# Weight tiles split earlier, a modulation ring kept through two stages, tables loaded in the opening, and the MLP's gate on VectorE, in a two-layer transformer kernel

## The reference, cut to what matters

```python
mx = jnp.split(cond_x @ ada_w[i] + ada_b[i], 6, axis=-1)
hx = modulate(rms_norm(x, g[0]), mx[0], mx[1])
...
x = x + mx[2] * rms_norm(ox, g[1])
x = x + mx[5] * rms_norm(sq_relu_mlp(modulate(rms_norm(x, g[2]), mx[3], mx[4]),
                                     ff_w1[i], ff_w2[i]), g[3])
```

## Time and profile before

| | us |
|---|---|
| three runs | 3427.12, 3431.72, 3430.05 |
| median | 3430.05 |
| the profiled execution | 3428.0 |
| its span, first to last instruction | 3426.2 |
| its mean granted clock | 0.982 |

### The profile page before, as it was taken

The page is one execution under the profiler, slowest core; times in us unless marked ns, Lnnn a source line. Parts: engine busy times, 40 slices in busy tenths (PEclk is TensorE's granted clock), DMA queues, the critical chain, the costliest instruction groups (busy, mean ns, idle before and its releaser), DMA issues. The chain is left out here.

```text
span 3426.2 us, 39368 instructions
## 1 busy us (share of the span) xinstructions
PE 3290.3 (96%) x15248; PEld 2428.1 (71%) x15248; DVE 1898.6 (55%) x2428; ACT 1285.7 (38%) x2110; POOL 695.5 (20%) x383
## 2 busy tenths in 40 slices
PE   6999999999999999999999999888999999999998
PEld 3664445555888888888999878653457788888886
DVE  3335444433756765664685534577685654445444
ACT  4333444445543323332454222552113533333232
POOL 0001777665431001300220100110012410002001
PEclk8999999999999999999999999999999999999999
DMA  5626333322454454543465311102413432333333
GB/s 221 238 100 236 65 61 78 85 54 73 152 169 131 140 171 137 172 148 94 155 194 160 119 44 39 45 38 106 183 31 117 135 129 93 98 94 125 117 96 105
DMA packets 146651, 406.64 MB, mean 119 GB/s; under 512 B 25498, under 2 KB 39610, under 8 KB 143649
## 3 DMA queue, kind: packets, MB, share of 16 engines
q1 hardware_dynamic: 146464, 404.11, 36.9%
HBM read 345.05 MB, written 58.92 MB: 118 GB/s over the span
## 5 line engine op out<-in xcount | busy, mean ns | idle before, releaser
L1734 PE MATMUL psum<-hid_high,w_high_and_low 128*128 128x512 f32 (+1 forms) x1536 | 416.6, 356 | 7.0 <-DVE hid_low L1983 4.9
L1717 PE MATMUL psum<-h_high,w_high_and_low 128*128 128x512 f32 (+1 forms) x1536 | 415.8, 356 | 0.0
L2005 POOL TENSOR_TENSOR squares_then_rstd_of_out<-squares_then_rstd_of_out,square_out 128x512 f32<-128x512 f32 (+1 forms) x69 | 105.4, 1528 | 1275.8 <-ACT square_out L1804 1275.8
L1789 ACT ACTIVATE w_high_and_low<-w_raw 128x1024 fp32r<-128x1024 f32 x226 | 238.7, 1056 | 326.5 <-PE psum L1734 228.1
L1887 DVE TENSOR_TENSOR w_high_and_low<-w_raw,w_high_and_low 128x1024 fp32r<-128x1024 f32 x226 | 283.3, 1254 | 83.2 <-ACT w_high_and_low L1789 82.4
L1415 POOL TENSOR_TENSOR probs_added<-probs_added,probs_turned 128x1024 f32<-128x1024 f32 x128 | 308.2, 2408 | 67.2 <-ACT probs_turned L1340 54.6
L1734 PEld LDWEIGHTS psum<-hid_high,w_high_and_low 128*128 128x128 f32 x1536 | 274.3, 190 | 50.3 <-DVE hid_low L1983 4.5
L1382 DVE TENSOR_REDUCE row_max<-psum 128x1 f32<-128x1280 f32 x120 | 179.0, 1492 | 229.1 <-PE psum L1278 137.2
L1717 PEld LDWEIGHTS psum<-h_high,w_high_and_low 128*128 128x128 f32 x1536 | 272.8, 189 | 43.8 <-issue 3.7
L1980 DVE TENSOR_TENSOR hid_high<-hid_relu_and_square 128x512 fp32r<-128x512 f32 (+1 forms) x160 | 113.8, 711 | 318.2 <-ACT hid_relu_and_square L1874 317.8
L1734 PE MATMUL psum<-hid_low,w_high_and_low 128*128 128x512 f32 (+1 forms) x768 | 272.3, 355 | 0.0
(11 more groups left out here) (490 smaller groups left out, 6704.8 us busy)
## 6 DMA issues: line engine op xcount, KB each, us to landing
w_raw<-in_ff_w_dram SPq DMA_DIRECT2D x320, 512.0 KB, 3.6
ada_ring<-in_ada_w_dram SPq DMA_DIRECT2D x12, 2048.0 KB, 15.2
ada_rows_in<-in_ada_w_dram SPq DMA_DIRECT2D x96, 256.0 KB, 3.6
w_raw<-in_w_out_dram SPq DMA_DIRECT2D x38, 512.0 KB, 3.6
scratch_spectra<-spectrum_out SPq DMA_DIRECT2D x32, 256.0 KB, 2.0
filter_ring<-scratch_spectra SPq DMA_DIRECT2D x16, 512.0 KB, 4.0
stream_in<-scratch_x SPq DMA_DIRECT2D x27, 256.0 KB, 4.1
w_raw<-in_w_hy_dram SPq DMA_DIRECT2D x12, 512.0 KB, 3.8
```

The lines of the kernel that those rows point to most:

```text
L1717: mm = pe.matmul(bank[:, 0:n], x[i % SLOTS][:, k, :], y[:, k, a:a + n], start=(k == 0 and m == 0), stop=(k == KT - 1 and m == 2))
L1734: mm = pe.matmul(bank[:, 0:n], x[i % SLOTS][:, 2 * k + half, :], y[:, k, 0:n], start=(k == 0 and m == 0), stop=(k == HT - 1 and m == 2))
L1789: act.activation(w_hi[i % SLOTS], raw[i % 2], ACT.Copy).then_inc(w_rounded, 1)
L2005: pool.tensor_tensor(acc_out[:, q % 2, 0:n], acc_out[:, q % 2, 0:n], sq_out[:, v % 2, 0:n], ALU.add).then_inc(added_out, 1)
```

## The change

Four edits. The first weight tiles are loaded ahead of the second chunk of x, rounded by ScalarE ahead of that chunk's squares, and split by VectorE inside the scaling of the chunks. One `Modulation` with one ring serves both stages: SyncE issues its loads of pieces 4 to 6 of the list in the opening, and the projection multiplies the first of them in step 0. `by_head`, `swap` and `cos_a` are loaded in the opening; `sin_a` remains in the projection, with a semaphore of its own. Pieces 10 and 11, the MLP's gate, leave the ring and become a first batch of `ModulationRows` in layer 0's MLP, whose gating waits for it.

```diff
-ADA_LATER = [(0, piece) for piece in range(4, ADA_PIECES)]
-ADA_IN_MLP = [(1, (2, 3), BOTH), (1, (0, 1), BOTH)] + [(1, (4, 5, 6, 7), LATENT), (1, (8, 9, 10, 11), LATENT)]
+ADA_LATER = [(0, piece) for piece in range(4, 10)]
+ADA_IN_MLP = [(0, (10, 11), BOTH), (1, (2, 3), BOTH), (1, (0, 1), BOTH)] + [(1, (4, 5, 6, 7), LATENT), (1, (8, 9, 10, 11), LATENT)]
...
                 ada.load(sp, 1)
+                for t in range(2):
+                    sp.dma_start(g.first_raw[:, t], d["w_qk"][t]).then_inc(w_first, 16)
                 load_x(1)
                 ada.load(sp, 2)
-                for t in range(2):
-                    sp.dma_start(g.first_raw[:, t], d["w_qk"][t]).then_inc(w_first, 16)
                 ada.load(sp, 3)
                 load_x(2)
+                for dst, src in ((g.by_head, "by_head"), (g.swap, "swap_a"), (g.cos_a, "cos_a")):
+                    sp.dma_start(dst[:], d[src]).then_inc(g.tabs_in, 16)
+                for i in range(NEEDED, NEEDED + ada.SLOTS):
+                    ada.load(sp, i)
...
                 scale(0, BACK)
-                scale(1, range(KT))
-                ada.bias(dve, 2)
-                split_off(0, FRONT)
-                split_off(1, FRONT)
                 for t in range(2):
                     dve.wait_ge(w_rounded, t + 1)
                     dve.tensor_tensor(g.first_low[:, t], g.first_raw[:, t], g.first_high[:, t], ALU.subtract).then_inc(w_split, 1)
+                scale(1, FRONT)
+                ada.bias(dve, 2)
+                scale(1, BACK)
+                split_off(0, FRONT)
+                split_off(1, FRONT)
                 ada.bias(dve, 3)
...
-                ada.load_selector(sp)
-                for dst, src in ((by_head, "by_head"), (swap, "swap_a"), (cos, "cos_a"), (sin, "sin_a")):
-                    sp.dma_start(dst[:], d[src]).then_inc(tabs_in, 16)
+                sp.dma_start(sin[:], d["sin_a"]).then_inc(sine_in, 16)
                 ring.load(sp, 2, qk_piece(2))
-                for i in range(ada.SLOTS):
-                    ada.load(sp, i)
                 for u, (t, a, n) in enumerate(units):
-                    if u + 1 >= ADA_FROM:
-                        ada.load(sp, u + 1 - ADA_FROM + ada.SLOTS)
+                    ada.load(sp, ADA_DONE + ada.SLOTS + u)
...
-                    ada.turn(pe, step - ADA_FROM - 1)
-                    if step >= ADA_FROM:
-                        ada.multiply(pe, step - ADA_FROM)
+                    if step:
+                        ada.turn(pe, ADA_DONE + step - 1)
+                    ada.multiply(pe, ADA_DONE + step)
...
-                dve.wait_ge(tabs_in, 64)
+                dve.wait_ge(tabs_in, 48)
+                dve.wait_ge(sine_in, 16)
...
                     if k == 0:
                         dve.wait_ge(rstd_out, q + 1)
+                        if ADA and q == C:
+                            dve.wait_ge(ada.folded, ada.folds_by(of_gate[-1]))
```

More of the change, by code:

```diff
@@ L152, in copy @@
             act.wait_ge(self.turned, i - len(self.banks) + 1)
-        act.activation(self.rows[:, i % len(self.banks), :], self.bank(i), ACT.Copy).then_inc(self.copied, 1)
+        act.activation(self.rows[:, i % 2, :], self.bank(i), ACT.Copy).then_inc(self.copied, 1)
     def turn(self, pe, i):
@@ L161, in turn @@
         for m in range(BANK // P):
-            mm = pe.matmul(self.bank(i)[:, 2 * m:2 * m + 2], self.rows[:, i % len(self.banks), m * P:(m + 1) * P], self.sel[:], start=True, stop=True)
+            mm = pe.matmul(self.bank(i)[:, 2 * m:2 * m + 2], self.rows[:, i % 2, m * P:(m + 1) * P], self.sel[:], start=True, stop=True)
         mm.then_inc(self.turned, 1)
@@ L596, in _ @@
                 for step in range(U + 3):
-                    ada.copy(act, step - ADA_FROM - 1)
+                    if step:
+                        ada.copy(act, ADA_DONE + step - 1)
                     if step < U and step % C == 1:
@@ L1535, in out_and_mlp @@
                 loads_at.setdefault(0 if done is None else min(i for i in rows_at if rows_at[i][-1] >= done) + 1, []).append(m)
[L1536 removed]
+            of_norm = [b for b, (of_layer, of_pieces, streams) in enumerate(ADA) if of_layer > layer and of_pieces[0] < 4]
+            of_gate = [b for b, (of_layer, of_pieces, streams) in enumerate(ADA) if of_layer == layer]
             bank_of = lambda i: g.ps[:, unit_of[i, "ada"] % BANKS, :]
@@ L3222, in build_program @@
         g.first_high, g.first_low = (tile_r(nc, g.first_ring, f"w_{x}", [P, 2, KT, P]) for x in ("high", "low"))
+        g.ada_memory = ExitStack()
+        g.by_head, g.swap = tile(nc, g.ada_memory, "ones_by_head", [P, P]), tile(nc, g.ada_memory, "swap_halves", [P, P])
+        g.cos_a, g.tabs_in = tile(nc, g.ada_memory, "cos_a", [P, TOK]), nc.alloc_semaphore("tables_in")
+        ada_sems = [nc.alloc_semaphore(n) for n in "ada_in0 ada_in1 ada_in2 sel_in made copied turned biased folded".split()]
+        g.ada = Modulation(nc, g, d, g.ada_memory, ada_sems, ADA_FIRST + ADA_LATER, (6, 7))
         opening(nc, g, d)
```

37 lines of the change are left out of this document (18 added, 19 removed).

## The result

The changed kernel takes 3435.85 us (median of 20 runs, 3432.20 to 3439.64) where the kernel before takes 3429.89 us (median of 20). The ratio is 1.0016, with a 95% interval of 1.0010 to 1.0022: slower by 6 us, small but clear of 1, inside the 0.2% that I had called no change, and inside the forecast's range. It is just outside the 4 us around 3431.5 us that I gave a chance of 0.55. The terms behind it were of both signs and most of them nearly as large as forecast. The profiled execution took 3434.41 us, its span 3432.6. One execution of a later kernel (e11) took 8391.69 us and is left out of every comparison.

What follows compares the result with a forecast made beforehand. TensorE, busy 96% of the span, was taken to bound the kernel. Terms of -1.8, +2.7, -14.45, +5.6, +10.05, +2.5, +2.0 and -5.1 summed to +1.5 us, 3431.5 us; eight-in-ten range 3423.5 to 3438.5.

Steps and rivals of the forecast that it cites:

- the 4 us around 3431.5 us: Whole kernel: the forecast time as summed, to be met within 4 us, chance 0.55.
- The bound: Whole kernel: TensorE is busy 96% of the span, so edits count only through its work or few waits.
- The opening (-1.8): Start of kernel: weights loaded and rounded earlier let PE's first product start at 48.6 us, 1.8 us sooner.
- T3 (+2.7): Projection's first product: modulation work fills the gap ahead of it without shortening it; the low clock costs 2.7 us.
- B + 14.1: Projection's first product placed 14.1 us behind the stage's start, against 14.0 before, without the clock's price.
- The ring after T3 and the two waits (-14.45 + 18.15): Projection after its first product: fewer multiplies and turns save 14.45 us; two late ring loads and low clock cost 18.15.
- The low clock: Projection's late ring loads: half-speed work costs 2.2 us within the second wait and 2.5 us behind it.
- the landing: Projection's ring loads: each lands 7.4 us after issue, with bounds of 5.0 and 15.2 us.
- The MLP (+2.0): Layer 0's MLP: VectorE's gate work hides in its waits; PE's extra sum and turn cost 2.0 us.
- The bank (-5.1): Start of project_mamba: a shifted PSUM bank removes the first product's wait and keeps the clock high, saving 5.1 us.
- The rival in which the wait stays: Start of project_mamba: VectorE's clearing or the second weight tile holds PE anyway; +5.1 us, 3436.6 us, chance 0.08.
- The sum: Whole kernel: all terms together give +1.5 us, 3431.5 us on the median, no change that shows.

Runs made afterwards that it cites:

- e11: The changed kernel with the ring's last two pieces multiplied in steps 6 and 8 instead of 4 and 5, SyncE's order untouched: 3413.48 us, ratio 0.9957.
- e10: e5 plus three unread TensorE products in the opening's gap, where PE waits for the later chunk's squares: 3407.53 us, ratio 0.9940.
- e5: e1 with the projection's head sum made ahead of the ring's turn and multiply in each step: 3411.68 us, ratio 0.9946.
- e7: The changed kernel with the ring's next load issued ahead of its unit's two stores, still behind the wait for the low part: 3436.46 us, ratio 1.0021.
- e2: The kernel before with only the third dt sum's PSUM bank changed, to bank 1: 3424.10 us, ratio 0.9984.
- e4: The kernel before with only the MLP's gate (last two pieces) moved from the ring to VectorE in layer 0's MLP: 3421.43 us, ratio 0.9974.
- e9: e4 with VectorE's additions for the gate cut to 64 of 512 columns, leaving out part of the computation: 3418.93 us, ratio 0.9973.
- e1: The changed kernel with the ring loads of the 9th and 10th piece issued ahead of the first store: 3417.45 us, ratio 0.9961.
- e3: The kernel before with by_head, swap and cos_a loaded in the opening, sin_a alone in the projection, ring of squares 4 deep: 3425.39 us, ratio 0.9985.

## Why the prediction was right or wrong

**The bound** was right: each edit counted where it moved PE's waits or its clock, and VectorE's and ScalarE's added work showed only through them.

**The opening (-1.8) was wrong; it measured -0.1.** The step that failed was "the squares, PE's sums and the root all come 2.5 us later". The sums came 2.5 us later and lasted 2.6 us longer, because the clock fell in the idle stretch that the later chunk made for PE. I had priced the clock at the first product and not here. e10 is the test: with that stretch filled the sum takes 7.03 us and the barrier comes 1.9 us sooner than in e5. Against the kernel before, e10's first product is 1.1 us sooner (49.32) and its barrier 1.4 (72.34), most of the forecast's 1.8. In e7, whose opening is that of the changed kernel, the clock stood until 29.4 and the sum took 8.62 us; the first product came at 49.96 and, with the clock up sooner behind it (0.67 in 52 to 54 us, 0.50 before), the barrier at 72.31. So a part of the term is there in some executions. The Trainium skill, TensorE: Matmul & The Clock Gate, Part 1, says that the point of change varies between runs; these traces agree (28.0 and 29.4 us under the same instructions).

One reading at the head of the prediction is wrong as well: `sin_a` is not PE's only long wait in the first 300 us. PE waits 11.0 us ahead of its first sum of squares, and 5.4 at the turn of the earlier trace rows. No edit touches the first of them.

**T3 (+2.7) was right in mechanism**: +3.3, the gap filled and not shortened, and the low clock in it (2.69 and 3.54 us for multiplies of 1.92). My order of events had it at B + 14.1 without the clock's price; e5 shows what held it there, the head sum behind two multiplies. The size is good to a microsecond or so only: in the profiled executions T3 lay 12.3 to 14.0 us behind the barrier where `sin_a` was waited for (before, e2, e4, e9), and 17.3 to 18.8 in the kernels with the ring kept in the changed kernel's order.

**The ring after T3 and the two waits (-14.45 + 18.15) were right in mechanism.** Forecast +3.7 from T3 to the stage's end, measured +3.1. e1 parts the two: without the late loads that stretch takes 96.03 us, 15.7 less than before, and the late loads add 18.8. That 18.8 is so near to 18.15 is partly luck, by two errors that offset each other. The idle time itself was forecast as 5.6 and 7.85 us (10.05 less the 2.2 of the clock), 13.45 together, and measured 6.63 and 9.38, 16.0 together. The low clock was put at 2.2 + 2.5 = 4.7 us, and 2.8 are left for it.

The mis-sized part of the waits is the landing. The first load was issued 13.2 us behind T3, as forecast; only its 7.4 us were too short. I had read them from the DMA engines' busy windows, and the loads took 8.1 and 9.0 (to 112.32 and 130.88). In the changed kernel too the DMA engines are nearly quiet (busy share 0.12 in 111 to 112 us) about a microsecond before PE starts. The view of the DMA issues puts the very load of the earlier trace rows at 9.2 us to its landing:

```profile
ada_ring<-in_ada_w_dram SPq DMA_DIRECT2D x1, 2048.0 KB, 9.2
```

So quiet DMA engines are not yet a landing. e1 and e11 show in two ways that these waits and what hangs on them are 18 to 22 us of the time. The estimate of 6.8 us by the Trainium skill, DMA: Bandwidth & Descriptors, section Anatomy of one DMA, was further off than the row.

**The MLP (+2.0) was mis-sized**: +4.3 in the changed kernel and 3.9 to 8.3 us in the profiled executions of the ten later kernels that have the gate there, the largest in e10 (-0.7 and +0.7 in e3 and e2, which have it not). The step that failed is "it hides there". Besides the sum and turn of 2.0 us, PE's waits for split weights grew from 3.6 to 5.1 us in the changed kernel, and e9 shows that the additions make these longer; one split alone is 1.1 us of it, as the last section shows. That is 1.5 of the missing 2.3 us. I had looked for the cost in the waits for `hid_low`, which are as long without the gate (7.1 us in e2). The remaining 0.8 us is within what executions differ by.

**The bank (-5.1) was right**: -4.8 here, -5.0 alone in e2. The rival in which the wait stays falls.

**The sum** +1.5 became +6.4: +1.7 from the opening, +2.3 from the MLP, +0.6 from T3, -0.6 behind it, +0.3 from the bank, and +0.6 in stretches without an edit. The range held because it was wide enough for the opening's 1.7 and the MLP's 2.3, and it had foreseen the cause of neither.

## What to carry to other kernels

A ring that runs one step ahead of its consumer works only while nothing that it must be issued behind depends on the step before. Look in the issuing queue for what stands ahead of each load, and follow that back: here a store, its low part, a head sum, and the very multiply that the previous load was late for. Before filling an idle stretch, see what it waits for and put that first (e5: 5.8 us). Where a load is moved back, ask whether PE's new idle stretch costs it the clock. And read a load's landing from its issue-to-landing row or from its consumer, not from the moment at which the DMA engines fall quiet (7.4 against 9.2 us here).

## What the runs showed of the hardware

The same split of a weight tile took 1.22 us in e2 and 2.31 us in e4, at the same step of the MLP. In both GpSimd adds squares beside it; the timelines differ in who starts first. e2, then e4:

```profile
897.48 1.22 DVE L1887 TENSOR_TENSOR w_high_and_low<-w_raw,w_high_and_low 128x1024 fp32r<-128x1024 f32 x1
...
897.70 2.15 POOL L2030 TENSOR_TENSOR squares_then_rstd_of_x<-squares_then_rstd_of_x,square_x 128x512 f32<-128x512 f32 x1 [2.07 <-ACT square_x L1846]
```

```profile
886.00 3.93 POOL L2033 TENSOR_TENSOR squares_then_rstd_of_x<-squares_then_rstd_of_x,square_x 128x512 f32<-128x512 f32 x2 [1.38 <-ACT square_x L1847]
...
886.47 2.31 DVE L1888 TENSOR_TENSOR w_high_and_low<-w_raw,w_high_and_low 128x1024 fp32r<-128x1024 f32 x1
```

In e2 VectorE began first and GpSimd's addition took 2.15 us (1.30 in a row a few us earlier); in e4 GpSimd began first and VectorE's split took 1.09 us more, which PE then waited for (1.27 us for `w_high_and_low`, 0.17 in the kernel before). The Trainium skill, SBUF — State Buffer, section SBUF: two separate sides, says that whichever of the two starts first, a VectorE operation with two inputs in SBUF or a GpSimd operation, keeps the shared port pair for its whole instruction; these rows agree. In e2 the weight tile arrived 0.7 us later against PE's products, ScalarE's squares behind its rounding came later too, and so did GpSimd's addition. In e9, where the tile came as early as in e4 and only the additions are shorter, VectorE reached the split 0.96 us behind the start of ScalarE's rounding (885.73) and not 2.12, ahead of GpSimd, and took 1.22 us again. I had not expected that 0.7 us in the arrival of one weight load, or one addition more on VectorE, decides it.
